# Half of the x sums from extra transposes, the log counts in fewer steps, the filler matmuls spread over all score units, and a new plan for the banded stage

## The reference, cut to what matters

```python
def token_mixer(x, w_in, b_forget, sinks, w_branch, w_gate, b_gate, w_out):
    (aq, ak, av, bq, bk, bv, cq, ck, cv, ciq, cik, ciw, dq, dk, dv, df) = jnp.split(x @ w_in, offsets, axis=-1)
    o_a = banded_attention(...)      # A: window of 128 keys, 8 heads on 2 key heads, sinks
    o_b = dilated_attention(...)     # B: (window, dilation) in (128, 1), (512, 4), (2048, 16)
    o_c = dsa_attention(...)         # C: score = sum_h iw[t,h] * relu(iq[t,h] . ik[s]), then top 256
    o_d = forgetting_attention(...)  # D: cumulative log forget gates
    gates = jax.nn.sigmoid(x @ w_gate + b_gate).reshape(b, L, N_BRANCH, D_MODEL)
    merged = jnp.sum(gates * proj, axis=2)      # proj: the four outputs times w_branch
    return merged @ w_out
...
x = layer_norm(DEEPNORM_ALPHA * x + token_mixer(x, ...)); then the same with conv_glu_ffn(x, ...)
```

## Time and profile before

| | |
|---|---|
| three runs | 2134.28, 2135.15, 2136.54 us (median 2135.15) |
| profiled execution | 2136.81 us, span 2135.0 us |
| PE busy | 2073.9 us, 97% of the span |
| DVE busy | 1558.0 us, 73% |
| ACT busy | 973.4 us, 46% |
| POOL busy | 934.7 us, 44% |
| granted TensorE clock, mean | 0.991 |

### The profile page before, as it was taken

The page is one execution under the profiler, slowest core; times in us unless marked ns, Lnnn a source line. Parts: engine busy times, 40 slices in busy tenths (PEclk is TensorE's granted clock), DMA queues, the critical chain, the costliest instruction groups (busy, mean ns, idle before and its releaser), DMA issues.

```text
span 2135.0 us, 28861 instructions
## 1 busy us (share of the span) xinstructions
PE 2073.9 (97%) x10350; PEld 1729.5 (81%) x10350; DVE 1558.0 (73%) x2596; ACT 973.4 (46%) x1752; POOL 934.7 (44%) x732
## 2 busy tenths in 40 slices
PE   8799999999999999999999999999999999999998
PEld 6578887888887888888887888878788888888887
DVE  5669888767687666698775766667877777775668
ACT  4443333655633565615743665432433333334541
POOL 5367762333322332322332333534765555555751
PEclk9999999999999999999999999999999999999999
DMA  4123332110042111041031000341566565558862
GB/s 129 41 86 117 104 111 78 21 31 27 14 148 60 50 41 38 22 167 30 21 105 44 11 21 21 119 157 49 159 188 202 182 196 172 158 196 306 276 208 94
DMA packets 197374, 224.27 MB, mean 105 GB/s; under 512 B 25704, under 2 KB 149608, under 8 KB 197232
## 3 DMA queue, kind: packets, MB, share of 16 engines
q1 hardware_dynamic: 194320, 212.43, 31.8%
q10 hardware_dynamic: 2912, 10.00, 1.3%
HBM read 164.17 MB, written 58.23 MB: 104 GB/s over the span
## 4 chain that ended last, share of the span: by engine, by line
PE 80%; DVE 11%; ACT 3%; issue 3%; POOL 2%; DMA 1%; ACTq 0%; DVEq 0%
PE pair L1315 13%; PE pair L894 13%; PE pair L1181 7%; PE obank L1315 5%; PE pair L878 5%; PE pair L1344 5%; PE obank L988 4%; PE chunk L967 4%; PE pair L939 3%; PE chunk L1344 3%; PE obank L1181 3%; PE pair L1274 3%; PE pair L940 3%; PE obank L1344 2%; DVE o_top L2327 2%
## 5 line engine op out<-in xcount | busy, mean ns | idle before, releaser
L2116 POOL TENSOR_TENSOR w_lo<-w_raw,w_hi 128x1024 fp32r<-128x1024 f32 x64 | 158.6, 2479 | 320.7 <-ACT w_hi L1608 320.5
L2517 DVE TENSOR_TENSOR pt_lo<-chunk,pt_hi 128x512 fp32r<-128x512 f32 (+1 forms) x272 | 173.7, 639 | 86.3 <-ACT pt_hi L1631 82.5
L1631 ACT ACTIVATE pt_hi<-chunk 128x512 fp32r<-128x512 f32 (+1 forms) x272 | 150.8, 555 | 171.3 <-PE chunk L967 169.9
L2164 POOL TENSOR_SCALAR prob<-prob,att 128x256 f32<-128x256 f32 (+4 forms) x172 | 117.9, 696 | 237.6 <-DVE att L2453 237.6
L894 PE MATMUL pair<-act_hi,w_hi 128*128 128x512 f32 x432 | 187.5, 434 | 1.1 <-DVE heads L2458 0.9
L894 PE MATMUL pair<-act_hi,w_lo 128*128 128x512 f32 x432 | 170.8, 395 | 0.0
L894 PE MATMUL pair<-act_lo,w_hi 128*128 128x512 f32 x432 | 170.2, 394 | 0.0
L2327 DVE TENSOR_SCALAR_CACHE_REDUCE o_top<-score,stat 128x384 uint8<-128x384 f32 (+1 forms) x186 | 166.6, 941 | 0.4
L988 PE MATMUL obank<-pt_hi,heads 128*128 128x256 f32 (+1 forms) x568 | 148.8, 286 | 1.9 <-DVE o_t L2525 1.2
L1727 ACT ACTIVATE prob<-prob,att 128x256 f32<-128x256 f32 (+4 forms) x172 | 120.5, 701 | 47.7 <-DVE att L2441 46.2
L988 PE MATMUL obank<-pt_lo,heads 128*128 128x256 f32 (+1 forms) x568 | 139.2, 281 | 0.0
(11 more groups left out here) (492 smaller groups left out, 5963.1 us busy)
## 6 DMA issues: line engine op xcount, KB each, us to landing
down_sums<-dn_sums SPq DMA_DIRECT2D x40, 512.0 KB, 6.3
w_raw<-in_w_in SPq DMA_DIRECT2D x37, 512.0 KB, 3.8
gates<-o_t SPq DMA_DIRECT2D x22, 512.0 KB, 2.9
up_raw<-in_w_up SPq DMA_DIRECT2D x22, 512.0 KB, 4.8
gate_raw<-in_w_ffn_gate SPq DMA_DIRECT2D x22, 512.0 KB, 6.0
hidden<-gelu_s SPq DMA_DIRECT2D x22, 512.0 KB, 3.4
dn_raw<-down_sums SPq DMA_DIRECT2D x44, 256.0 KB, 3.8
h_in<-down_sums SPq DMA_DIRECT2D x44, 256.0 KB, 4.7
```

The lines of the kernel that those rows point to most:

```text
L2116: nc.gpsimd.tensor_tensor(split_into(1, g), w_raw[:, g % 2, 0:kt * cols], split_into(0, g).bitcast(F32), ALU.subtract).then_inc(lo_ready, 1)
L2517: nc.vector.tensor_tensor(pt_lo[:, n % PT_SLOTS, 0:m], t[:, 0:m], pt_hi[:, n % PT_SLOTS, 0:m].bitcast(F32), ALU.subtract).then_inc(chunk_f ...
```

## The change

**x sums.** PE transposes the second half of x once more, in eight further groups (n = 16 to 23), two behind each of the first parts of the second column half of tile 0, while DVE makes the raw sums 7 and 4 straight from PSUM. POOL's 16 instructions go; POOL makes the lo parts of 5 and 6 instead (8 instructions), DVE those of 7 at once and of 4 at the head of gates. ACT makes the hi parts of 5, 6 and 7 before it takes ik out of PSUM, those of 7 once all eight groups have been taken; only those of sum 4 stay within the scores.

**Log counts.** 14 steps instead of 20: 5 ahead of q of branch B (before 11), 9 behind as before.

**Fillers.** `SCORE_PARTS` places all 48 parts at the score units: 5 ahead, one behind each of the first three units and two behind each of the next 20.

**Banded stage.** In `BESIDE[A]` four parts leave iterations 4, 5 and 6 and stand in 7 to 9, where there are now eight; `AHEAD[A]` is 8 instead of 4, so eight parts of the tile after the next are made before pair 0 (before four) and the last pair makes eight instead of twelve. The first half of q0 is taken in iteration 2 instead of 3.

**Output weights.** ACT makes one more hi part of w_out ahead of the split of merged tile 6, and one less at the head of outproj.

```diff
-SCORE_PARTS = (5, 1, 1, 1, 1, 1, 1, 1, 1, 1, 2, 1, 2, 1, 2, 1, 2, 1, 1, 1, 1, 1, 1, 1, 0)
+SCORE_PARTS = (5,) + (1,) * 3 + (2,) * 20 + (0,)
...
-          A: ((0, 1), (0, 2), (0, 2), (1, 0), (1, 2), (2, 1), (2, 2), (3, 2), (4, 2), (4, 2),
-              (5, 0), (6, 1), (8, 1), (9, 2), (9, 2), (9, 2)),
+          A: ((0, 1), (0, 2), (0, 2), (1, 0), (1, 2), (2, 1), (2, 2), (3, 1),
+              (7, 1), (7, 2), (8, 0), (8, 1), (8, 2), (9, 0), (9, 1), (9, 2)),
...
-AHEAD = {A: 4}
+AHEAD = {A: 8}
...
-    at = {A: ((3, "q0", 0), (5, "q0", 1), (6, "q1", None))}.get(
+    at = {A: ((2, "q0", 0), (5, "q0", 1), (6, "q1", None))}.get(
...
                     pe.wait_ge(x_taken, 2 * NTOK)
+                    again = iter(range(2 * NTOK, 3 * NTOK))
                     for tile in first:
                         for _part in tile:
-                            pass
+                            for n in itertools.islice(again, 2):
+                                turn_x(n)
...
-                    act.wait_ge(x_taken, 2 * NTOK)
-                    for p in X_SUMS[:2]:
+                    for p in X_SUMS[:3]:
+                        act.wait_ge(x_taken, (3 if p == 7 else 2) * NTOK)
                         for k in range(4):
                             x_sums_hi(p, k)
...
-                        while ring.n < ring_at["outproj",]:
+                        while ring.n <= ring_at["outproj",]:
                             ahead()
...
-                    for _tile in range(3):
+                    for _tile in range(2):
                         ahead()
...
-                for k in range(4):
-                    h11, l11, h12, l12 = (x_block(at, part, k).bitcast(F32) for at in (11, 12) for part in range(2))
-                    t7, t4_k = x_sum_raw(7, k), x_sum_raw(4, k)
-                    steps_of = told(t7, x_sum_raw(6, k), h11), told(t4_k, h12, x_sum_raw(6, k))
...
+                for p in X_SUMS[:2]:
+                    if p == 6:
+                        pool.wait_ge(x_taken, 3 * NTOK)
+                    for k in range(4):
+                        pool.wait_ge(xs_hi, 4 * X_SUMS.index(p) + k + 1)
+                        nc.gpsimd.tensor_tensor(x_sum(p, 1, k), x_sum_raw(p, k), x_sum(p, 0, k).bitcast(F32),
+                                                ALU.subtract).then_inc(xs_lo_early, 1)
...
+                for last, dil in ((513.0, 4), (4095.0, 16)):
+                    own(nc.vector.tensor_scalar(di, dist[:], last, None, ALU.min))
                     yield
+                    own(nc.vector.tensor_scalar(di, di, dil - 1, 24, ALU.bitwise_and, ALU.logical_shift_left))
                     yield
+                    own(nc.vector.scalar_tensor_tensor(count, di.bitcast(F32), 0.0, count, ALU.is_equal, ALU.add))
                     yield
...
+                    for n in range(2 * NTOK, 3 * NTOK):
+                        j, c = n // 2 - NTOK, n % 2
+                        block = x_bank(n).rearrange("p (k t) -> p k t", k=4)
+                        dve.wait_ge(x_turned, n + 1)
+                        dve.wait_ge(x_taken, n)
+                        if c == 0:
+                            minus(x_sum_block(7, j), x_sum_block(6, j), block).then_inc(x_taken, 1)
+                        else:
+                            minus(x_sum_block(4, j), block, x_sum_block(6, j)).then_inc(x_taken, 1)
+                    for k in range(4):
+                        x_sums_lo(7, k)
...
-                        counted(11)
+                        counted(5)
```

More of the change, by code:

```diff
@@ L1 @@
+import itertools
 import math
@@ L1020, in attention @@
                         pe.wait_ge(*staged_all)
-                    fill(2)
+                    fill(AHEAD.get(br, 4) // 2)
                     pe.wait_ge(*staged_all)
-                    transpose_tokens(stage(br), lambda n: fill(2 * n))
-                elif br == A and pr == 0:
-                    fill(AHEAD[br] // 2)
+                    transpose_tokens(stage(br), lambda n: fill(AHEAD.get(br, 4) // 2 * n))
                 for g in range(len(stream) + 2):
@@ L1905, in _ @@
                             nc.scalar.activation(prob[:, unit % 2, 0:n], src[:, 0:n], ACT.Relu).then_inc(relu_done, 1)
-                            if 0 <= unit - XS_FIRST < 8:
-                                act.wait_ge(xs_raw, unit - XS_FIRST + 1)
-                                x_sums_hi(X_SUMS[2 + (unit - XS_FIRST) % 2], (unit - XS_FIRST) // 2)
+                            if 0 <= unit - XS_FIRST < 4:
+                                x_sums_hi(4, unit - XS_FIRST)
                             if unit == LAST_EARLY_SPLIT - 1:
@@ L2165, in normalise, with x_sums_lo @@
                                             att_stat(3, u), 1.0, ALU.mult, ALU.mult).then_inc(prob_ready, 1)
[L2167 to L2182 removed]
+            def x_sums_lo():
+                for p in X_SUMS[:2]:
[5 more added lines that the diff above has]
+                                                ALU.subtract).then_inc(xs_lo_early, 1)
             def pool_minus(dst, a, b, op=ALU.subtract):
@@ L2217, in _ @@
                         nc.gpsimd.tensor_scalar(sink_neg[:], sink[:], -1.0, None, ALU.mult).then_inc(consts_ready, 1)
-                        pool.wait_ge(x_taken, 2 * NTOK)
+                        x_sums_lo()
                     elif step[0] != "iw":
                         split_weights()
-                    for _part in range(XS_PARTS.get(step[:2], XS_PARTS.get(step[0], 0))):
-                        next(sums_of_x, None)
                 elif step[0] == "gates":
@@ L2765, in _ @@
                 elif kind == "iq":
-                    for k in range(4):
-                        dve.wait_ge(xs_hi, 4 * step[1] + k + 1)
-                        if X_SUMS[step[1]] == 6:
-                            dve.wait_ge(xs_raw, 2 * k + 2)
-                        x_sums_lo(X_SUMS[step[1]], k)
                     k = 1 - step[1]
@@ L2836, in _ @@
                 elif kind == "gates":
-                    for i, p in enumerate(X_SUMS[2:]):
-                        for k in range(4):
-                            dve.wait_ge(xs_hi, 8 + 2 * k + i + 1)
-                            x_sums_lo(p, k)
+                    for k in range(4):
+                        x_sums_lo(4, k)
                     dve.wait_ge(filler_taken, len(FILLER_GATES))
```

40 lines of the change are left out of this document (11 added, 29 removed).

## The result

The changed kernel takes 2158.27 us (median of four runs, 2154.66 to 2161.32) where the kernel before takes 2135.14 (2134.28 to 2136.54): 1.0107 times as long, 95% interval 1.009 to 1.0125. Forecast were 2149.3 us and a range up to 2157. The profiled execution has a span of 2159.5 us, 24.5 more than that of before; forecast were 14.2 more. PE's mean granted clock fell from 0.991 to 0.984.

A forecast was written before the change was run, and what follows sets the result against it. PE was taken as busy 2073.9 of 2135.0 us, with DVE, ACT, DVE pacing the banded stage up to q1. Terms +0.7 - 2.1 + 18.5 - 2.9 = +14.2 gave a 2149.3 us median; 8-in-10 range 2133 to 2157.

The forecast's parts named there:

- DVE sets the pace there: Banded stage, iterations 4 to 6: removing parts there buys nothing, since PE would only wait longer for heads.
- each part behind q1 costs its own 0.69 us: Banded stage: four parts moved behind DVE's q1 extraction add 2.76 us of the 4.25 forecast for each of three transitions.
- the second rival: Banded stage: only part of the backlog reaches the path, 1.1 us per transition; sum +1.8, 2137 us; chance 0.17.
- The start of the stage: Banded stage, ahead of pair 0: four more parts made there cost +2.8 us.
- the clock's step: Banded stage: longer waits ahead of q1 bring half clock to all three transitions instead of two, +2.8 us (0 to +3).
- near 30 us: Banded stage: length of the pair periods given as a sign that the forecast is right.
- Start and scores: Kernel start to gates: first score 3.0 us sooner, but PE idles ahead of gates; +0.7 us (-3.0 to +5).
- the relation of last relu and first weights: Ahead of gates: POOL and ACT make the weights only after the last relu, taking 8.0 us; PE idles 9 us.
- Log counts: Branch B's k heads: six fewer DVE steps shrink PE's 2.4 us wait to about 0.35, -2.1 us (0 to -2.4).
- Output weights: Output projection: PE's 2.9 us wait for the last weights goes, -2.9 us (0 to -2.9).
- PE paced the stage: Banded stage: moved parts fill PE's pauses and two half-clock stretches go, -10.7 us, in all -15, 2120; chance 0.10.
- the start is worse: Kernel start: ik's extraction 7.5 us late, two half-clock pauses, nothing regained; +5 instead of +0.7, some 2154; chance 0.13.

The follow-up runs named there:

- run 1: Kernel before with only the banded stage's part of the change (AHEAD 8, parts moved, q0's first half in iteration 2): 2157.96 against 2137.21 us, ratio 1.0092.
- run 7: Kernel before with AHEAD 6, two parts instead of four moved behind q1's extraction in the banded stage: 2147.72 us, +9.2, ratio 1.0046.
- run 12: Kernel before with the banded stage's part alone, all eight parts placed behind iteration 7's transposes and products: 2153.16 against 2136.24 us, ratio 1.0077.
- run 4: Kernel before with the new SCORE_PARTS (closed-up fillers) alone: 2142.13 us, +4.9, ratio 1.0022.
- run 5: Kernel before with the shorter log counts alone: 2137.58 against 2138.49 us, ratio 1.0002.
- run 6: Kernel before with the earlier output weights alone: 2134.70 against 2138.49 us, ratio 0.9981.
- run 8: Kernel before with AHEAD 2, two parts fewer behind q1's extraction in the banded stage: 2138.02 us, -0.5, ratio 0.9996.
- run 3: Kernel before with the x sums from extra transposes alone, fillers placed as before: 2138.34 us, ratio 1.0001.
- run 2: Changed kernel with the banded stage's part undone: 2135.09 us against the kernel before's 2137.21, ratio 0.9981.
- run 10: Kernel before with the x sums alone, but ik taken out of PSUM before sum 7's hi parts: 2136.04 against 2136.24 us, ratio 0.9998.
- run 13: Kernel before with the x sums, ik first, and the next weights' splits on ACT and POOL moved ahead too: 2140.75 against 2141.47 us, ratio 0.9996.
- run 15: Kernel before with x sums (ik and weight splits first), shorter log counts and earlier output weights: 2133.08 against 2141.47 us, ratio 0.9962.
- run 14: Kernel before with eight top-k steps moved from branch B's merge to branch A's: 2142.11 against 2141.47 us, ratio 1.0012.
- run 16: Kernel before with x sums (ik and splits first), log counts, output weights, and top-k steps moved to A's merge: 2133.80 us, ratio 0.9973.

## Why the prediction was wrong

- **The direction and the main mechanism held, the banded stage's two terms did not.** "DVE sets the pace there" and "behind q1" is what runs 1, 7 and 12 show: more behind q1 costs, in the order of how much was moved. The stage was forecast at +18.5; the trace has +20.8 and run 1's median +20.8. That this is close is luck. The forecast was 15.7 of parts and waits, and the trace has 11.6 more of idle PE; the forecast for half clock was +2.8, and it cost 9.2. So the step "each part behind q1 costs its own 0.69 us" was too dear (in run 12 four more parts cost 7.6 instead of 11): some of it is absorbed, as the second rival had it in kind, and where is left open. The start of the stage was too cheap by 0.8 (the first q1 comes 3.6 us later, not 2.8). And the clock's step failed in its size: I priced one more stretch like the two of before, 6.8 us long each, but there are four of 6.8 to 10.3 us. Pair by pair this hides again: 33.5 and 32.2 us, where the terms give 26.07 + 4.25 + 2.8 = 33.1. (The "near 30 us" that I gave as a sign left the clock out.)
- **Start and scores: mis-sized, +3.0 instead of +0.7.** Two steps failed. The four lo parts of sum 7 on DVE were left out of the chain to the copy (the diff puts them ahead of ik's), which cost 2 of the 3 us that I had credited at the first score. And the relation of last relu and first weights was right (9.41 us of idle PE, 9 forecast), but both lie 2 us later. The fillers by themselves cost 4.9 us by run 4's median, near the +5 of my bound, and 2.7 in its trace.
- **Log counts: the step failed, -0.6 in the trace and nothing in run 5's ratio instead of -2.1.** I took six steps of DVE off the path without asking where its next wait is. They stood ahead of q's lo part, which waits for ACT and PE; only 0.56 us came through (PE's wait went from 2.45 to 1.89), and a step behind it grew from 0.69 to 2.39 us beside POOL's weight split. A half-clock stretch right behind then took 1.6. It is no cost of this edit: 10 of the 12 profiles with the old log counts have that stretch near 370 us, and 2 of the 6 with the new ones. The profile of before, which I had to go by, is one of the two without.
- **Output weights: right**, -2.9 forecast; -4.1 in the trace, -3.8 in run 6. That it is more fits the clock: 7 of the 12 profiles with the old order have a half-clock stretch between 1410 and 1425 us, none of the 6 with the new one.
- **The merge of branch B: put at nothing, +5.5.** Nothing was changed there. It is what put the time out of the range, together with the terms above. The change need not be its cause: up to this merge the kernel before and those of runs 1, 6, 7, 8 and 12 are the same code, and two of these six profiles have the long wait (runs 1 and 7) and four don't. By medians on a common chip the parts add up to 20.8 - 2.1 = 18.7 us, and the kernel before in its lower times (2134 to 2138) is what the first comparison had beside it. So some of the 23.1 us may be which executions of before it met; the range was missed by 1.3.

The rival "PE paced the stage" is refuted by run 1. Of "the start is worse", ik comes as late as it says (PE waits 7.7 us in run 3), but by itself that costs nothing at the gates; what costs is the closed-up fillers of run 4, in addition to the banded stage rather than in its place. The forecast should have carried a term, or a wider range, for stages that the change only shifts in time and that differ from execution to execution.

## What to carry to other kernels

Before crediting a shortened chain on an engine, look for that engine's next wait: what is taken out ahead of it only lengthens the wait (log counts, ik first, and the parts that left iterations 4 to 6). Price the waits of a stage and its time at half clock as two terms, and compare each with the trace, since a sum that fits can hide two that don't. Work that has no deadline is worth most where the path's engine would otherwise wait, so fillers belong behind the last score and not closed up within the loop. And a stage in which a helper engine has half a microsecond of slack is a risk for every change that arrives there at another time.

## What the hardware showed

**One short instruction goes with 3 to 5.5 us.** In B's merge DVE is busy without a pause and PE waits 0.47 us. A top-k step there has DVE instructions of 128x6 elements, 0.17 us alone. The timelines of DVE and POOL, first of the kernel before:

```profile
613.52 2.40 POOL L2116 TENSOR_TENSOR w_lo<-w_raw,w_hi 128x1024 fp32r<-128x1024 f32 x1 [2.79 <-ACT w_hi L1608]
...
614.59 1.35 DVE L2347 TENSOR_SCALAR stat<-stat 128x6 uint32<-128x6 f32 x1
...
633.13 0.17 DVE L2348 SCALAR_TENSOR_TENSOR stat<-stat 128x6 uint32<-128x6 uint32 x1
...
634.08 2.41 POOL L2116 TENSOR_TENSOR w_lo<-w_raw,w_hi 128x1024 fp32r<-128x1024 f32 x1 [8.08 <-ACT w_hi L1608]
...
644.20 0.50 PE L878 MATMUL pair<-act_hi,w_hi 128*128 128x512 f32 x1 [0.47 <-DVE mid L2888]
```

and of the changed kernel:

```profile
618.45 2.39 POOL L2119 TENSOR_TENSOR w_lo<-w_raw,w_hi 128x1024 fp32r<-128x1024 f32 x1 [3.75 <-ACT w_hi L1610]
...
618.58 2.29 DVE L2340 TENSOR_SCALAR stat<-stat 128x6 uint32<-128x6 f32 x1
...
638.06 2.40 POOL L2119 TENSOR_TENSOR w_lo<-w_raw,w_hi 128x1024 fp32r<-128x1024 f32 x1 [7.09 <-ACT w_hi L1610]
638.09 2.38 DVE L2341 SCALAR_TENSOR_TENSOR stat<-stat 128x6 uint32<-128x6 uint32 x1
...
651.38 0.80 PE L879 MATMUL pair<-act_hi,w_hi 128*128 128x512 f32 x1 [3.68 <-DVE mid L2878]
```

DVE's instruction ends with POOL's (620.87 and 620.84). The weights' transfer landed a microsecond later, POOL began 0.13 us ahead of DVE's step instead of 1.07, DVE lost 0.94 us more, and so it met POOL's split again 20 us later, which it had passed by 0.8 us before (a meeting at 624 us, 2.1 us long, is in both traces); PE waits 3.68 us and falls to half clock. Of the 14 profiles whose merge has the steps of before, nine (the changed kernel's and runs 1, 2, 4, 5, 7, 10, 13 and 15) show a wait of 3.5 to 3.7 us, and five (before, 3, 6, 8, 12) one of 0.5 to 1.2; the four runs with fewer steps have none. That the two groups of times of the kernel before (some 2137 and 2142 in runs 13 to 16) are these two cases fits, and is not shown: only one of its executions was profiled. Nor does any run here move the weights' transfer alone; that the late transfer brings the third meeting is read from these two traces. The Trainium skill, "SBUF — State Buffer", section "SBUF: two separate sides", says that GpSimd and the vector engine share a port pair under an exclusive lock: where the vector engine's instruction is of a kind that needs the pair, whichever starts first has it for the whole instruction, and the other is blocked. The traces agree: POOL had started first each time, and the short instruction ends with POOL's.

**Half clock is no function of one wait.** At 372.03 us of the changed kernel PE waited 1.89 us and then fell to half clock; before it waited 2.45 us at the same place and did not. AHEAD 6 has more waits than AHEAD 4 and no half clock at its three transitions in the profiled execution, where AHEAD 4 has it at two. The traces can say what a stretch costs (2.8 us for the 6.8 us at a transition of before), but not whether the next version will have it or how long it will be.
